# First branch of a two-layer hybrid block: new unit order, one-bank accumulation, alternating PSUM banks, and attention steps placed between half units

## The reference

```
# branch A (latent attention): low-rank q and k/v, rope on 64 shared columns
qa  = (_rmsnorm(a_cq, a_g_cq) @ a_w_uq).reshape(b, s, 8, 128 + 64)
kva = (_rmsnorm(a_ckv, a_g_ckv) @ a_w_ukv).reshape(b, s, 8, 128 + 128)
qn = _rmsnorm(qa[..., :128]);  qr = _rope(_rmsnorm(qa[..., 128:]))
kn = _rmsnorm(kva[..., :128]); kr = _rope(_rmsnorm(a_kr))
scores = qn.kn + qr.kr  ->  masked softmax  ->  times v
# branch B (differential attention): two softmax maps per head, a = p0 - lam * p1,
# output normalised per head.  Branch C: chunked band attention with a bias.
y = sum_n sigmoid(gate_n) * ((o_n * silu(z_n)) @ w_branch[n]);  x = x + y @ w_out
```

## Time and profile before

| | |
|---|---|
| median of three executions | 3345.94 us |
| the profiled execution's own time | 3338.77 us |
| its span, first to last instruction | 3336.6 us |
| mean granted TensorE clock | 0.987 |
| busy: TensorE, VectorE, ScalarE | 97%, 63%, 51% |
| HBM read over the span | 171 GB/s |
| period of an A pair (of a B pair, of a C pair) | 44.3 us (75.6 us, 72.3 us) |

### The profile page before, as it was taken

The page is one execution under the profiler, slowest core; times in us unless marked ns, Lnnn a source line. Parts: engine busy times, 40 slices in busy tenths (PEclk is TensorE's granted clock), DMA queues, the critical chain, the costliest instruction groups (busy, mean ns, idle before and its releaser), DMA issues.

```text
span 3336.6 us, 53239 instructions
## 1 busy us (share of the span) xinstructions
PE 3235.7 (97%) x18180; PEld 2784.5 (83%) x18180; DVE 2091.7 (63%) x2644; ACT 1715.8 (51%) x2220; POOL 0.2 (0%) x4
## 2 busy tenths in 40 slices
PE   8999999999999899999999999989899999999999
PEld 6888888888888787788888888878778888888888
DVE  5577566666667656566666555765656666655566
ACT  4585444444454455555555555535555555555554
POOL 0000000000000000000000000000000000000000
PEclk9999999999999899999999999999999999999999
DMA  6555655555656454365555555555445555565555
GB/s 191 184 182 182 196 189 169 178 178 167 192 161 211 130 176 122 118 200 164 163 176 174 174 176 179 176 177 166 125 136 185 166 165 164 174 186 181 181 172 174
DMA packets 570275, 572.18 MB, mean 171 GB/s; under 512 B 26305, under 2 KB 565953, under 8 KB 570177
## 3 DMA queue, kind: packets, MB, share of 16 engines
q1 hardware_dynamic: 570176, 570.94, 55.1%
HBM read 568.77 MB, written 2.10 MB: 171 GB/s over the span
## 4 chain that ended last, share of the span: by engine, by line
PE 93%; DVE 3%; ACT 2%; issue 1%; DMA 0%; ACTq 0%; DVEq 0%; SPq 0%
PE pg L462 86%; PE pa L598 2%; PE pa L576 1%; ACT hl L732 1%; PE pa L616 1%; PE pa L542 1%; DVE hl L990 1%; PE pa L617 1%; PE pa L606 0%; PE pa L554 0%; DVE work L997 0%; DVE mix L1083 0%; DMA raw<-w_o 0%; ACT corr L743 0%; DVE hT L1091 0%
## 5 line engine op out<-in xcount | busy, mean ns | idle before, releaser
L462 PE MATMUL pg<-hT,hl 128*128 128x512 f32 x12480 | 2229.5, 339 | 32.0 <-DVE hT L1091 17.3
L462 PEld LDWEIGHTS pg<-hT,hl 128*128 128x128 f32 x12480 | 1911.8, 189 | 319.2 <-issue 14.6
L990 DVE TENSOR_TENSOR hl<-raw,hl 128x1024 fp32r<-128x1024 f32 x1076 | 1273.6, 1221 | 338.9 <-ACT hl L732 332.2
L732 ACT ACTIVATE hl<-raw 128x1024 fp32r<-128x1024 f32 x1076 | 1096.9, 1053 | 322.6 <-PE pg L462 301.7
L743 ACT ACTIVATE corr<-pg 128x512 f32<-128x512 f32 x320 | 188.6, 590 | 985.7 <-PE pg L462 981.1
L462 PE MATMUL pg<-uT,hl 128*128 128x512 f32 (+1 forms) x2560 | 468.8, 345 | 16.2 <-DVE work L997 11.4
L462 PEld LDWEIGHTS pg<-uT,hl 128*128 128x128 f32 x2560 | 401.9, 194 | 78.9 <-DVE work L997 14.4
L997 DVE TENSOR_TENSOR work<-pg,corr 128x512 f32<-128x512 f32 (+1 forms) x186 | 125.1, 676 | 336.5 <-ACT corr L743 336.2
L462 PE MATMUL pg<-hl,hT 128*128 128x512 f32 (+1 forms) x1792 | 326.1, 341 | 0.0
L462 PEld LDWEIGHTS pg<-hl,hT 128*128 128x128 f32 x1792 | 274.5, 188 | 46.2 <-issue 7.6
L997 DVE TENSOR_TENSOR gat<-pg,corr 128x512 f32 (+1 forms) x72 | 49.7, 691 | 218.8 <-ACT corr L743 218.8
(11 more groups left out here) (147 smaller groups left out, 1246.3 us busy)
## 6 DMA issues: line engine op xcount, KB each, us to landing
raw<-w_in SPq DMA_DIRECT2D x792, 512.0 KB, 4.6
raw<-w_br SPq DMA_DIRECT2D x96, 512.0 KB, 4.3
raw<-w_out SPq DMA_DIRECT2D x64, 512.0 KB, 4.7
raw<-w_rnn SPq DMA_DIRECT2D x32, 512.0 KB, 4.6
raw<-w_o SPq DMA_DIRECT2D x32, 512.0 KB, 5.2
raw<-w_att SPq DMA_DIRECT2D x16, 512.0 KB, 3.5
raw<-w_uq SPq DMA_DIRECT2D x16, 384.0 KB, 3.5
tab<-tabs SPq DMA_DIRECT2D x5, 896.0 KB, 7.3
```

The costliest lines, as they stand in the source:

```text
L462: return nc.tensor.matmul(out, lhsT, rhs, start=start, stop=stop, skip_group_check=True)
L732: nc.scalar.activation(hl4[:, j % 2, 0, a], raw[:, bass.ds(j % 2 * UC + a.start, UC // 2)], ACT.Copy)\
L990: tt(hl4[:, j % 2, 1, a], raw[:, bass.ds(j % 2 * UC + a.start, UC // 2)], hl4[:, j % 2, 0, a].bitcast(F32), ALU.subtract).then_inc(lo_done, 1)
```

## The change

The work of a pair in branch A is reordered and its small products are accumulated differently; in A and B, attention steps are put between the two halves of a unit (`h6` is half 0 of unit 3, `h7` its half 1, and so on).

- Branch A, units: queries (unit 0), first half of the depth of the first gate chunk (unit 1), keys and values (unit 2), the second half of the first gate chunk (unit 3), the second gate chunk (units 4, 5). Query and key/value weights both use slot 0 now; each half of them is placed at the start of a half slot, and the splits of the key/value unit are 512 wide instead of 1024.
- `three_terms`: queries, keys and values are each accumulated in one set of 256 columns by three matmuls with 256 moving columns. Four outputs then fit in two banks. They are emptied by a VectorE `tensor_copy`, without `copy_corr` and without `join`. The chunks of a pair fall from 6 to 5.
- Even pairs use banks 0, 1 for queries, keys/values and the second gate chunk and banks 2, 3 for the first gate chunk; odd pairs the other way round. The loop over pairs of branch A therefore holds two pairs in its body and runs twice.
- The sigmoid of z moves from one 128x2048 step ahead of the pairs to a 128x512 step in each pair, with its two table loads.
- The squares of q and k start when the keys are out; the rope part is normalised and its semaphore given first; the scores run all four products of the unrotated part before they wait for the rotated one.
- The lines of the diff show `EVENTS` of A and B, then A of `ACT_EVENTS`, then A and B of `DVE_EVENTS`.
- Branch B: `t1`, `p1` and `n0-1` move between half units. Branch C and the dilated attention keep their order.

```diff
-    "A": events("u0-2 norm u3 rot u4 s0-1 u5 t0-1 p0-1"),
-    "B": events("u0-4 norm u5-6 s0 u7-8 t0 s1 u9 p0 u10 t1 p1 u11 n0-1"),
+    "A": events("u0-2 h6 norm h7 rot h8 s h9-10 t0-1 h11 p0-1"),
+    "B": events("u0-4 norm u5-6 s0 u7-8 t0 s1 u9 p0 h20 t1 h21 p1 h22 n0-1 h23"),
...
+    "A": events("u0-1 q u2 h6 norm h7-8 s0-1 h9-10 t0-1 h11 p0-1"),
+    "A": events("u0-2 h6 norm h7 rot h8 s0-1 x0-1 h9-11 p0-1 lo0-1"),
+    "B": events("u0-4 norm rot u5-6 s0 x0 u7-8 s1 x1 u9 h20-22 n0-1 h23 lo0-1"),
...
     if kind == "A":
-        return {0: [0, 1], 1: [2, 3], 3: [4], 5: [5]}
+        return {0: [0], 2: [1, 2], 3: [3], 5: [4]}
...
-                    load(u, 0, w_uq[...], 4 * 384)
-                    load(u + 1, 1, w_ukv[...], 2 * 512)
-                    for j in range(4):
-                        wide2(u + 2 + j, j, GATE + (2 * p + j // 2) * CH, 1024 * (j % 2))
+                    load(u, 0, w_uq[...], 4 * 384, UC // 2)
+                    wide2(u + 1, 1, GATE + 2 * p * CH, 0)
+                    load(u + 2, 0, w_ukv[...], 2 * 512, UC // 2)
+                    wide2(u + 3, 1, GATE + 2 * p * CH, 1024)
+                    for j in range(2):
+                        wide2(u + 4 + j, j, GATE + (2 * p + 1) * CH, 1024 * j)
...
+            def three_terms(out, xh, xl, yh, yl, start, stop):
+                mm(out, xh, yh, start, False)
+                mm(out, xh, yl, False, False)
+                return mm(out, xl, yh, False, stop)
+
+            def queries(b, u):
+                wh, wl = (w.rearrange("p h (k n) -> p h k n", n=384) for w in apart_view(0, 768))
+                for out, a in ((pg3[:, b, 0:S], 0), (pg3[:, b, S:], P), (pg3[:, b + 1, 0:S], 2 * P)):
+                    for k in range(4):
+                        w = [x[:, k // 2, k % 2, a:a + P] for x in (wh, wl)]
+                        ins = three_terms(out, *w, u3[:, 8 + k, 0:S], u3[:, 8 + k, S:], k == 0, k == 3)
+                ins.then_inc(half_done, 2)
+
+            def scores_with_rope(l, p):
...
+                for e in range(2):
+                    for tq in (1, 0):
+                        piece(e, tq, qk_l[:, e, :], qk_l[:, 2 + e, :], tq == 1, False)
+                pe.wait_ge(kr_ready, l + 1)
+                pe.wait_ge(roped, 4 * l + p + 1)
...
-                        hi(u, j + 2, short=kind == "A" and j >= 4)
+                        hi(u, n + 2, halves, 512 if n == 0 else UC // 2)
+                        if n == 0:
+                            z_sigmoid(z3[:, bass.ds(2 * p, 2), :], nt3[:, 5:7, :], C_L + l * LC_N + LC["A"] + 2)
+                    elif what == "q":
+                        act.wait_ge(evac_done, c + 4)
+                        act.wait_ge(u_ready, 2 * pi)
+                        nc.scalar.activation(nt3[:, 0:5, :], qk_l[:, 0:5, :], ACT.Square).then_inc(sq_ready, 1)
...
-                act.preload_act_table(ACT.Sigmoid)
-                act.wait_ge(evac_done, cl_ + 8 + 2)
-                nc.scalar.activation(g3[:, 0:8, :], z3, ACT.Sigmoid).then_inc(a_zs, 1)
-                exp_table()
...
+                        if n == 0:
+                            dve.wait_ge(half_done, 2 * u + 2)
+                            nc.vector.tensor_copy(qk_l[:, 0:2, :], both[0])
+                            nc.vector.tensor_copy(qk_l[:, 4:5, :], both[1][:, 0:1, :]).then_inc(evac_done, 1)
+                        elif n == 2:
+                            gate_z(z3[:, bass.ds(2 * p, 2), :], nt3[:, 5:7, :], PAIRS + 12 * l + p + 1)
+                            dve.wait_ge(a_part, 4 * l + p + 1)
+                            nc.vector.tensor_copy(qk_l[:, 2:4, :], both[0]).then_inc(evac_done, 1)
+                            dve.wait_ge(half_done, 2 * (u + 2) + 2)
+                            nc.vector.tensor_copy(v_l, both[1]).then_inc(evac_done, 1)
...
-                dve.wait_ge(a_zs, l + 1)
-                steps.done(tt(z3, z3, g3[:, 0:8, :], ALU.mult))
```

More of the change, by code:

```diff
@@ L79 @@
 ACT_EVENTS = EVENTS | {
-    "A": events("u0-2 norm u3-4 s0-1 u5 t0-1 p0-1"),
-    "B": events("u0-4 norm u5-6 s0 u7-8 t0 s1 u9 p0 u10 t1 p1 u11 n0-1 o0-1"),
+    "A": events("u0-1 q u2 h6 norm h7-8 s0-1 h9-10 t0-1 h11 p0-1"),
+    "B": events("u0-4 norm u5-6 s0 u7-8 t0 s1 u9 p0 h20 t1 h21 p1 h22 n0-1 h23 o0-1"),
 }
@@ L482, in token_major, with apart_view, unit @@
                 return ins
+            def apart_view(j, n):
+                return [hl4[:, j % 2, h, :].rearrange("p (s n) -> p s n", s=2)[:, :, 0:n] for h in range(2)]
             def both_view(j, n):
                 return hl4[:, j % 2, :, :].rearrange("p h (k n) -> p k h n", n=n)
-            def unit(u, j, c, cj, op, first, last, form="f", subs=2, ready=None):
+            def unit(u, j, c, cj, op, first, last, form="f", subs=2, ready=None, halves=(0, 1)):
                 base = 0 if first else 8
@@ L492, in unit @@
                 wh, wl = split_view(j, CH)
-                for h in range(2):
+                for h in halves:
                     pe.wait_ge(lo_done, 2 * u + h + 5)
-                    if first and h == 0:
+                    if first and h == 0 and c is not None:
                         pe.wait_ge(evac_done, c + 1)
@@ L1258, in target, with gate_z, pair @@
                 return g3[:, bass.ds(4 * p + 2 * (cc - 4), 2), :]
-            def pair(kind, l, p, u, c):
+            def gate_z(z, zt, n):
+                dve.wait_ge(z_sig, n)
+                steps.done(tt(z, z, zt, ALU.mult))
+            def pair(kind, l, p, u, c, bank=0):
                 pi = pi_of(kind, l, p)
@@ L1316, in pair @@
                         tt(ut[:, :, S:], o, ut[:, :, 0:S].bitcast(F32), ALU.subtract).then_inc(u_ready, 1)
-            PAIR_STEPS = {"1": 17, "A": 5, "B": 14, "C": 5}
+            PAIR_STEPS = {"1": 17, "A": 6, "B": 14, "C": 5}
             def pairs(kind, l, u0, c0):
-                with dve.Fori(0, PAIRS) as p:
-                    mark = steps.loop(p, PAIR_STEPS[kind])
-                    pair(kind, l, p, u0 + p * units(kind), c0 + p * CHUNKS[kind])
-                steps.end(mark, PAIRS)
+                turns = 2 if kind == "A" else 1
+                with dve.Fori(0, PAIRS // turns) as i:
+                    mark = steps.loop(i, PAIR_STEPS[kind] * turns)
+                    for n in range(turns):
+                        p = i * turns + n
+                        pair(kind, l, p, u0 + p * units(kind), c0 + p * CHUNKS[kind], 2 * n)
+                steps.end(mark, PAIRS // turns)
             pairs("1", 0, U_P1, C_P1)
```

245 lines of the change are left out of this document (132 added, 113 removed).

## The result

The changed kernel takes 3259.77 us (median of four executions, 3256.04 to 3262.70) against 3345.82 us (3344.37 to 3346.19): a ratio of 0.9743, 95% interval 0.9726 to 0.9760, 86 us or 2.6% faster. The forecast was 3284 us with a range of 3272 to 3302 us: the direction and most of the mechanism were right, the size was 24 us short, and the time lies 12 us under the range. The profiled execution took 3256.04 us, its span went from 3336.6 to 3254.2 us, so 82.4 us are to be found in the two traces; the other 3.6 us of the 86 lie between the medians and the profiled executions.

What follows compares the result with a forecast made beforehand. TensorE, busy 97% of the span, was taken as the bound, so gains come from its waits and low clock. A stages 47.1 us plus branch B 14.5 us made 61.6 us: 3345.9 to 3284 us, range 3272 to 3302 us.

Steps and rivals of the forecast that it cites:

- All three waits of the earlier trace: TensorE waits to vanish: 5.46 us where A pairs begin, 28.0 us before weighted values, 4.1 us before the branch product.
- The walk: Step-by-step check of one A pair for TensorE waits; margins 1.7, 0.6, 0.3, nil and 1.6 us.
- the one place without margin: Rotated scores in the A pair, wanted at about 26.1 us: margin nil, up to 0.5 us may appear.
- returns: TensorE going back from a small step to units: 0.13 us each, 0.8 us per A pair, 1.0 us over B.
- Rival 3: Each table load holds ScalarE as long again: 2.0 us per A pair, 16 us, 3300 us; chance 0.02.
- rival 4: Three matmuls into the same 256 columns run slower; at 0.28 us each 74 us, 3358 us; chance 0.03.
- rival 1: New waits in the A pair at squares, rotation, rotated scores: 12 us back, 3296 us; chance 0.18.
- rival 2: The clock stays low at times in the A stages: 15 us come back, 3299 us; chance 0.05.
- rival 5: The edit does nothing for the A pairs; B alone gives 14.5 us, 3331 us; chance 0.01.
- the sum of the A pair: TensorE's steps in one A pair, many carried over unchanged: 39.6 us if it waits nowhere, four pairs 158.4 us.
- own lower edge, 3275 us: Low end of the forecast's own spread: 0.116 us per matmul, 4 us, and free returns, 4 us.
- the clock of 0.72 at the queries: A pair's queries after 2.30 us idle: 5.55 us at clock 0.72, 1.55 us lost, to go with the wait.

Runs made afterwards that it cites:

- experiment 8: Changed kernel with the sigmoid of z as one 128x2048 step ahead of the A pairs again: 3268.18 us against 3337.00 for the kernel before, ratio 0.9787.
- experiment 6: Changed kernel with branch A's transposes and weighted values together after the last half unit: 3277.23 us against 3337.00 for the kernel before, ratio 0.9819.
- experiment 10: Changed kernel with the three event strings of branch B as before: 3274.23 us against 3345.24 for the kernel before, ratio 0.9792.
- experiment 9: Changed kernel with the three outputs as inner loop of the 36 query matmuls: 3258.81 us against 3337.00 for the kernel before, ratio 0.9767.
- Experiment 1: Kernel before with only branch A's score products grouped by weight shape, 128-row then 64-row: 3318.57 us against 3345.24, ratio 0.9917.
- experiment 2: Changed kernel, scores still grouped, with the wait for the rotated part ahead of all of them: 3267.72 us against 3345.24 for the kernel before, ratio 0.9771.
- experiment 3: Changed kernel with score products alternating between shapes and the rotated-part wait ahead of all (mixed scores): 3309.36 us against 3345.24 for the kernel before, ratio 0.9899.
- experiment 4: Changed kernel with branch A's scores one half unit later, grouped, transposes and values together: 3268.76 us against 3341.53 for the kernel before, ratio 0.9778.
- experiment 5: Changed kernel with branch A's scores one half unit later, shapes alternating, transposes and values together: 3287.33 us against 3341.53 for the kernel before, ratio 0.9834.

## Why the prediction fell short

**What held.** All three waits of the earlier trace rows went where the text said: a gate unit between queries and keys (experiment 8: nearly all of it without the moved sigmoid), a half unit between transposes and values (experiment 6: 1.44 us come back, 1.9 expected), `h23` behind `n0-1` in B. The walk found the one place without margin, and the trace has its wait there, 0.26 us; square, rotation and weighted values do not wait. Queries and keys took 0.122 and 0.120 us per matmul from start to start, 0.126 predicted. B was put at 14.5 us, of which 12.7 us were waits less returns; experiment 10 measures 11.5 us. Rival 3 falls with the sigmoid that starts 0.01 us after its table load; rival 4 with experiment 9; rival 1 with the waits; rival 2 with the clock of 1.00; rival 5 with the 33 us of each A stage.

**What failed.** The step is the sum of the A pair, "The rest is unchanged: norm 1.72 + 0.43 us, rotation 0.43 us (two 256-column matmuls like those of L579), scores 3.98 us", and in it above all the scores. The pair came to 36.89 in place of 39.62 us, 2.73 us too long (ends of matmuls are modelled, so each part may be off by 0.1 us):
- scores 3.98 against 2.45 us: 1.53 us. I had read that the four unrotated products now come first and used it for the wait alone. It also turns seven changes between 128-row and 64-row weights into one, and puts the 64-row products of the two heads beside each other. Experiment 1 against the kernel before, 2 against 3 and 4 against 5 each show 1.8 us for the order alone (3.98 to 2.17 in 1, 4 and 5); in the changed kernel 0.28 us of wait and turn-around comes back between the two groups.
- weighted values 1.85 against 1.30 us: 0.55 us. I had added 0.35 us of on-paper overlap that is the entry into the queries, which the queries' own time has too. Another 0.16 us was low clock: behind the same idle time the step takes 1.50 us in the kernel before and 1.34 us in experiment 1.
- units, returns and rotation 30.99 against 30.33 us: 0.66 us. The queries took 0.16 us less than booked, keys and values 0.14 us, and the returns 0.4 us and not 0.8. Of them only the one behind the scores is dear, 5.85 against 5.56 us for 32 matmuls, and it is a change of weight shape too; the others cost at most 0.06 us.

The forecast's own lower edge, 3275 us, held 8 us for faster matmuls and free returns and nothing for the scores, and so the range missed.

The ledger of the 82.4 us, beside the 61.6 us of the forecast: the A stages give 33.05 + 33.65 = 66.7 us, where 45.5 were booked, and that is the miss. From the branch product behind them to the first norm of C's pairs the changed kernel is 15.4 us shorter (1406.30 to 1831.54 against 1373.00 to 1788.18, 2511.88 to 2933.54 against 2434.70 to 2851.06), where 16.2 were booked: 11.5 us by experiment 10, the rest mostly the low clock behind the last A pair and at the end of the B pairs of layer one, 1.65 and 1.76 us. 0.3 us are left.

**Right in size, wrong in cause: the clock.** I took the clock of 0.72 at the queries to be the price of the 2.30 us idle time, and its end as part of that wait's. Experiment 1 keeps the idle time at 2.27 us and has 1.00 in seven pairs of eight, where the kernel before has 1.00 in one; experiment 6 has 1.44 us and 1.00; the mixed scores with 1.52 us ahead have 0.58. The Trainium skill, "TensorE: Matmul & The Clock Gate", section "Why this matters for your kernels", names idle gaps between bursts of matmuls as what brings the clock down. The traces agree for the 5.46 us waits at the start of the A pairs, with a clock of 0.60 and 0.51 behind them in the kernel before and no score product near:

```profile
1235.39:1239.93 4.54, 4.54 (x20) 4.15 (x21) 3.24 (x4) 0.60 (x1) 0.00 (x0) 0.60 0.36 94
...
2340.71:2345.00 4.29, 4.29 (x16) 3.90 (x17) 3.16 (x4) 0.60 (x1) 0.00 (x0) 0.51 0.31 74
```

For shorter gaps the length alone doesn't tell:

| idle time | score products near it | low clock |
|---|---|---|
| 2.30 us, kernel before | alternating, a unit ahead of it | 7 of 8 pairs |
| 2.27 us, experiment 1 | grouped, a unit ahead of it | 1 of 8 |
| 2.0 to 2.1 us, end of the B pairs (before, 1, 10) | none near | 1 of 6 times |
| 1.50 to 1.64 us, experiment 3 | alternating, right behind it | 4 of 8 |
| 1.50 to 1.64 us, experiment 2 | grouped, right behind it | 0 of 8 |
| 1.44 us, experiment 5 | alternating, a unit ahead of it | 0 of 8 |
| 1.44 us, experiments 4 and 6 | grouped, a unit or more ahead of it | 0 of 16 |

The change removed both the idle time and the alternation, so the forecast got the clock back without having its cause. The 1.76 us I booked for the end of B stood in layer one of the kernel before alone. Layer two has the same wait and a clock of 1.00, and so has experiment 10; so `h23` can't be credited with them.

**Still open.** What the clock needs to fall isn't settled by these runs: with 1.5 to 1.64 us directly ahead of alternating products it fell in four pairs and not in four others, with one trace of each of these kernels. Nor does a run undo the one-bank accumulation or the order of units by itself; their share of the A stage is read from the waits that are gone.

## What to carry to other kernels

A reordering of matmuls is a change of cost even if their number and sizes stay: look at which weight shapes follow each other, since here six changes fewer between 128-row and 64-row weights, and 64-row products of two heads next to each other, saved 1.8 us per pair and, with an idle time of 2.3 us left in, 1.5 us of clock on top in most pairs. Put a half unit of independent matmuls between a step and its dependent one rather than beside both; 2.8 us of cover is enough for a ScalarE split and copy. And when a row of before is carried into the sum as unchanged, check that its neighbours are unchanged too.

## What the runs showed that was not expected

- Grouping 16 score matmuls by weight shape in the kernel before gave 26.7 us (20 to 35), with nothing else edited; the whole change gives 86 us.
- Eight matmuls on 64-row weights, four in rows 0:64 and four in rows 64:128, take 0.86 us; eight on 128-row weights with the same moving columns take 1.31 us.
- Whether the clock is halved did not follow from the length of an idle time alone: 2.27 us with grouped products ahead had a clock of 1.00 behind it in seven pairs of eight, 1.52 us with alternating ones behind it had 0.58, and those scores took up to 7.1 instead of 2.17 us.
- A VectorE copy of 128x512 from PSUM takes 0.69 us, no less than the add of a PSUM and an SBUF operand of that size (0.69 us): so what the one-bank form saves per copy is ScalarE's part (0.60 us for 128x512) and the hand-over, not VectorE's time.
